# Strassen pairs of the FFNs: U2, U3 and P5 + P3 accumulate in PSUM, with ScalarE's copies in between, in place of VectorE's sums

## The reference, cut to what matters

```
def swiglu(x, w_gate, w_up, w_down):
    return (jax.nn.silu(x @ w_gate) * (x @ w_up)) @ w_down
x = x + FFN_RESIDUAL * swiglu(rms_norm(x, g[0]), ffn_w_gate[layer, 0], ffn_w_up[layer, 0], ffn_w_down[layer, 0])
```

## Time and profile before

| | |
|---|---|
| median of 3 runs | 1956.07 us |
| span of the profiled execution | 1954.0 us; the page gives no other time of it |
| TensorE busy | 1948.1 us (100%) |
| VectorE busy | 1397.9 us (72%) |
| ScalarE busy | 851.6 us (44%) |
| GpSimd busy | 527.3 us (27%) |
| DMA | 265.92 MB, mean 136 GB/s |

### The profile page before, as it was taken

One profiled execution on the slowest core, in us unless ns is written; L12 is line 12 of the kernel. 1 busy time (PEld: TensorE's weight loads), 2 busy tenths in 40 slices (PEclk: granted clock), 3 DMA queues, 4 the chain that ended last, 5 costly groups with the idle time before them and its releaser, 6 DMA issues.

```text
span 1954.0 us, 28996 instructions
## 1 busy us (share of the span) xinstructions
PE 1948.1 (100%) x11722; PEld 1707.3 (87%) x11722; DVE 1397.9 (72%) x1882; ACT 851.6 (44%) x1230; POOL 527.3 (27%) x394
## 2 busy tenths in 40 slices
PE   9999999999999999999999999999999999999999
PEld 7999998877789999988999998877777888999997
DVE  7877776554588877768877776773458657877773
ACT  6443333535554344345433444442546345333431
POOL 1322222142223322223322322200015413322221
PEclk9999999999999999999999999999999999999999
DMA  6556663351346666545666653232200235666653
GB/s 211 155 164 171 173 168 95 119 181 55 88 126 176 174 172 167 147 129 145 178 166 172 181 151 114 97 96 88 76 1 1 87 116 160 177 173 168 178 141 107
DMA packets 112469, 265.92 MB, mean 136 GB/s; under 512 B 10321, under 2 KB 22865, under 8 KB 112337
## 3 DMA queue, kind: packets, MB, share of 16 engines
q1 hardware_dynamic: 92336, 225.72, 35.3%
q0 software_dynamic: 19856, 38.28, 12.5%
q10 hardware_dynamic: 144, 0.09, 0.0%
HBM read 259.32 MB, written 4.72 MB: 135 GB/s over the span
## 4 chain that ended last, share of the span: by engine, by line
PE 98%; DVE 1%; DMA 0%; issue 0%; ACT 0%; SPq 0%; POOL 0%; DVEq 0%
PE BANKS L656 12%; PE BANKS L658 12%; PE BANKS L657 12%; PE BANKS L579 11%; PE BANKS L580 11%; PE BANKS L581 11%; PE BANKS L709 6%; PE BANKS L710 6%; PE BANKS L711 6%; PE BANKS L1022 2%; PE BANKS L850 1%; PE BANKS L852 1%; PE BANKS L851 1%; PE BANKS L999 1%; PE BANKS L1005 1%; PE BANKS L813 1%
## 5 line engine op out<-in xcount | busy, mean ns | idle before, releaser
L656 PE MATMUL BANKS<-BF,ASH 128*128 128x256 f32 x876 | 248.0, 283 | 0.0
L658 PE MATMUL BANKS<-BF,ASL 128*128 128x256 f32 x876 | 247.9, 283 | 0.0
L657 PE MATMUL BANKS<-BFL,ASH 128*128 128x256 f32 x876 | 247.9, 283 | 0.0
L579 PE MATMUL BANKS<-XH,HI 128*128 128x512 f32 x624 | 245.7, 394 | 0.7 <-DVE XL L1593 0.3
L1657 DVE TENSOR_TENSOR LO<-RING,HI 128x1024 fp32r<-128x1024 f32 (+2 forms) x204 | 216.3, 1060 | 41.2 <-ACT HI L1160 39.9
L580 PE MATMUL BANKS<-XL,HI 128*128 128x512 f32 x624 | 243.2, 390 | 0.0
L581 PE MATMUL BANKS<-XH,LO 128*128 128x512 f32 x624 | 243.0, 389 | 0.0
L1173 ACT ACTIVATE TMP<-TMP 128x512 f32<-128x512 f32 x88 | 55.7, 633 | 406.4 <-DVE TMP L1686 406.4
L2262 POOL TENSOR_TENSOR TMP<-TMP,RSTD 128x512 f32<-128x512 f32 x88 | 132.0, 1499 | 365.3 <-ACT TMP L1173 365.3
L2254 POOL DMA_DIRECT2D ASR<-gu_dram x73 | 88.1, 1219 | 387.5 <-DMA ASR<-gu_dram 381.5
L709 PE MATMUL BANKS<-HH,DHI 128*128 128x512 f32 x488 | 190.7, 391 | 0.0
(11 more groups left out here) (249 smaller groups left out, 4875.5 us busy)
## 6 DMA issues: line engine op xcount, KB each, us to landing
RING<-gu_dram SPq DMA_DIRECT2D x174, 512.0 KB, 3.9
ASR<-gu_dram SPq DMA_DIRECT2D x146, 256.0 KB, 2.9
ASR<-gu_dram POOLq DMA_DIRECT2D x73, 512.0 KB, 6.9
DRAW<-down_dram SPq DMA_DIRECT2D x40, 512.0 KB, 3.7
RING<-oin_dram SPq DMA_DIRECT2D x32, 512.0 KB, 3.5
RING<-down_dram SPq DMA_DIRECT2D x32, 384.0 KB, 3.2
DRAW<-down_dram SPq DMA_DIRECT2D x24, 384.0 KB, 3.7
RING<-ein_dram SPq DMA_DIRECT2D x16, 512.0 KB, 3.6
```

Source lines behind the costliest of these rows:

```text
L579: pe.matmul(PS[bank][:], HI[j][:, c], hi(k), start=(n == 0), stop=False)
L656: pe.matmul(out, w_hi[:, c], x_hi(k), start=(k == 0), stop=False)
L657: pe.matmul(out, w_hi[:, c], x_lo(k), start=False, stop=False)
L658: last = pe.matmul(out, w_lo[:, c], x_hi(k), start=False, stop=(k == 3))
```

## The change

What it does:

- TensorE's order becomes P1, P5, P6, P2, P7, P3, P4. P1, P6 and P7 accumulate in one half bank, bank 4 or 5 by turns with p (`chain`), so that it holds P1, then U2, then U3. P5 starts the up bank's high half, and P3 accumulates on it. P2 goes to the same bank's low half without a start flag. P4 goes as before to the gate bank's low half.
- ScalarE copies the half bank after each step: P1 to MID[0] (as before), U2 to MID[1] (`copy_six`), U3 to MID[2] (`copy_seven`); and P5 from the up bank's high half to the gate bank's high half (`copy_five`), from PSUM to PSUM.
- TensorE waits for P1's copy before P6 (as before, now one product behind P1 and not three), for P5's copy before P2, and for U2's copy before P7. It no longer waits for VectorE's `mid_five` before P4, nor for the last pair's `mid_three` before P1; instead P1 waits for U3's copy of two pairs ago (in an FFN's first pair, of the last one).
- VectorE's `mid_two`, `mid_five` and `mid_three` are gone. `whole_up` adds MID[0:2] = (P1, U2) to the up bank, `whole_gate` adds MID[2] = U3 to the gate bank.
- ScalarE's order for a middle pair becomes: copy of P1, split of up weights, copy of P5, split of gate weights, copy of U2, two splits of sums, copy of U3, early split, silu, copy of h. In an FFN's first pair the copy of P5 stands behind the copy of the previous pair's h, and early split and up weights' split stand ahead of the copy of U2. In a pair behind one without an early part, the copy of P5 comes ahead of the copy of h and the copy of U2 behind it and behind the up weights' split.
- SyncE's load of the pair sums' inputs two pairs ahead waits for P7 of the pair (`seven_done`) instead of P5, since P7 is now the later of the two that read the tiles it overwrites.
- XH and XL, BF and BFL, ASH and ASL are views of common tiles at the same addresses as before. MID has six half tiles instead of four, and the mixer region grows from 34 to 35 tiles.

```diff
@@ SyncE, block_ffn
-                        sp.wait_ge(five_done, block_count(f, n // 2 - 2) + 1)
+                        sp.wait_ge(seven_done, block_count(f, n // 2 - 2) + 1)
                         load_pair(f, n // 2)
@@ TensorE, block_ffn
                 def block(p):
...
+                    chain = PS[4 + p % 2][:, 0:TH_]
...
-                    if g:
-                        pe.wait_ge(mid_made, 5 * g - 2)
-                    product(PS[5][:, low], HI[up][:, left], LO[up][:, left], plain(0, 0)).then_inc(one_done, 1)
+                    if g >= 2:
+                        pe.wait_ge(seven_copied, g if p == PLAIN[f] else g - 1)
+                    product(chain, HI[up][:, left], LO[up][:, left], plain(0, 0), True, True).then_inc(one_done, 1)
                     pe.wait_ge(sum_lo, 2 * g + 1)
-                    product(PS[4][:, low], *summed(p, 0), form(1)).then_inc(seven_done, 1)
-                    product(gate_bank[:, high], *summed(p, 1), form(0)).then_inc(five_done, 1)
+                    product(up_bank[:, high], *summed(p, 1), form(0), True, True).then_inc(five_done, 1)
                     pe.wait_ge(one_copied, g + 1)
                     pe.wait_ge(sum_lo, 2 * g + 2)
-                    product(PS[5][:, low], *summed(p, 2), form(2)).then_inc(six_done, 1)
-                    product(up_bank[:, low], HI[up][:, right], LO[up][:, right], plain(4, 0)).then_inc(unit_done, 1)
-                    product(up_bank[:, high], *summed(p, 3), plain(4, 1)).then_inc(three_done, 1)
-                    pe.wait_ge(mid_made, 5 * g + 2)
+                    product(chain, *summed(p, 2), form(2), False, True).then_inc(six_done, 1)
+                    pe.wait_ge(five_copied, g + 1)
+                    product(up_bank[:, low], HI[up][:, right], LO[up][:, right], plain(4, 0),
+                            False, True).then_inc(unit_done, 1)
+                    pe.wait_ge(six_copied, g + 1)
+                    product(chain, *summed(p, 0), form(1), False, True).then_inc(seven_done, 1)
+                    product(up_bank[:, high], *summed(p, 3), plain(4, 1), False, True).then_inc(three_done, 1)
                     pe.wait_ge(lo_ready, n + 2)
                     product(gate_bank[:, low], HI[gate][:, right], LO[gate][:, right], form(3)).then_inc(unit_done, 1)
@@ ScalarE, block_ffn
                     act.wait_ge(one_done, g + 1)
                     if g:
-                        act.wait_ge(mid_made, 5 * g - 1)
-                    act.activation(MID[:, 0, :], PS[5][:, 0:TH_], ACT.Copy).then_inc(one_copied, 1)
+                        act.wait_ge(up_added, g)
+                    act.activation(MID[:, 0, :], PS[4 + p % 2][:, 0:TH_], ACT.Copy).then_inc(one_copied, 1)
+
+                def copy_five(p):
+                    up_bank, gate_bank = block_banks(p)
+                    act.wait_ge(five_done, block_count(f, p) + 1)
+                    act.activation(PS[gate_bank][:, TH_:T], PS[up_bank][:, TH_:T], ACT.Copy).then_inc(five_copied, 1)
+
+                def copy_six(p):
+                    act.wait_ge(six_done, block_count(f, p) + 1)
+                    act.activation(MID[:, 1, :], PS[4 + p % 2][:, 0:TH_], ACT.Copy).then_inc(six_copied, 1)
+
+                def copy_seven(p):
+                    g = block_count(f, p)
+                    act.wait_ge(seven_done, g + 1)
+                    if g:
+                        act.wait_ge(gate_added, g)
+                    act.activation(MID[:, 2, :], PS[4 + p % 2][:, 0:TH_], ACT.Copy).then_inc(seven_copied, 1)
...
                     copy_one(p)
                     if p == first:
                         h_high(p - 1)
+                        copy_five(p)
                         early_split(p)
                     elif not has_early(f, p - 1):
+                        copy_five(p)
                         h_high(p - 1)
                     if nxt:
                         split(2 * nxt, whole)
-                        split(2 * nxt + 1, right)
+                        if p > first and has_early(f, p - 1):
+                            copy_five(p)
+                            split(2 * nxt + 1, right)
+                            copy_six(p)
+                        else:
+                            copy_six(p)
+                            split(2 * nxt + 1, right)
                         sums_split(nxt, 0)
                         sums_split(nxt, 1)
                     else:
                         split(NU, late)
+                        if has_early(f, p - 1):
+                            copy_five(p)
+                        copy_six(p)
                         split(NU + 1, late)
+                    copy_seven(p)
                     if p == ALONE[f]:
                         early_split(p + 1)
@@ VectorE, block_ffn
-                def mid_two(p):
...
-                def mid_five(p):
...
-                def mid_three(p):
...
                 def whole_up(p):
...
-                    dve.wait_ge(mid_made, 5 * g + 2)
+                    dve.wait_ge(six_copied, g + 1)
                     dve.wait_ge(three_done, g + 1)
-                    dve.tensor_tensor(bank, bank, MID[:, 0:2, :], ALU.add).then_inc(mid_made, 1)
+                    dve.tensor_tensor(bank, bank, MID[:, 0:2, :], ALU.add).then_inc(up_added, 1)
...
                         if leads(f, p):
-                            if p > first:
-                                early_split(p)
-                            mid_two(p)
-                            mid_five(p)
-                            mid_three(p)
-                            if p == first:
-                                early_split(p)
+                            early_split(p)
                         sums_second(nxt)
                         sums_third(nxt)
                         dve.wait_ge(sum_made, 2 * block_count(f, nxt) + 2)
                         split(2 * nxt, whole)
-                        if not leads(f, p):
-                            mid_two(p)
-                            mid_five(p)
-                            mid_three(p)
                         if not leads(f, p):
                             early_split(p)
```

More of the change, by code:

```diff
@@ L189, in trunk @@
         hr0 = region("h_region", 16 * TB)
-        e0 = region("mixer_region", 34 * TB)
+        e0 = region("mixer_region", 35 * TB)
         tmp0 = region("tmp_region", 8 * TB)
@@ L201, in trunk @@
         TMP = at("TMP", [P, 8, T], tmp0, 0)
-        XH = at("XH", [P, KX, T], xr0, 0, F32R)
-        XL = at("XL", [P, KX, T], xr0, 8 * TB, F32R)
+        XHL = at("XHL", [P, 2, KX, T], xr0, 0, F32R)
+        XH, XL = XHL[:, 0], XHL[:, 1]
         HH = at("HH", [P, 8, T], hr0, 0, F32R)
@@ L247, in trunk @@
         WT = [TMP[:, 0, :], TMP[:, 1, 0:3 * P], WT2[:], TMP[:, 1, 3 * P:T]]
-        BF = at("BF", [P, 4, 4, TH_], e0, 0, F32R)
+        FORMS = at("FORMS", [P, 2, 2, 16 * TH_], e0, 0, F32R)
+        BFHL = FORMS[:, :, 0, :].rearrange("p m (k i t) -> p m k i t", k=4, i=4)
+        BF, BFL = BFHL[:, 0], BFHL[:, 1]
+        ASL, ASH = (FORMS[:, m, 1, :].rearrange("p (b i c) -> p b i c", b=2, i=4) for m in range(2))
         BFR = at("BFR", [P, 4, 4, TH_], e0, 16 * TB)
-        BFL = at("BFL", [P, 4, 4, TH_], e0, 16 * TB, F32R)
         ASR = at("ASR", [P, 2, 4, T], e0, 8 * TB)
-        ASL = at("ASL", [P, 2, 4, T], e0, 8 * TB, F32R)
-        ASH = at("ASH", [P, 2, 4, T], e0, 24 * TB, F32R)
-        MID = at("MID", [P, 4, TH_], e0, 32 * TB)
+        MID = at("MID", [P, 6, TH_], e0, 32 * TB)
         DRAW = at("DRAW", [P, KMAX * P], tmp0, 4 * TB)
@@ L317, in trunk @@
             sem(n) for n in ("one_done", "five_done", "six_done", "seven_done"))
-        one_copied, mid_made, three_done = (sem(n) for n in ("one_copied", "mid_made", "three_done"))
+        one_copied, five_copied, six_copied, seven_copied, three_done = (
+            sem(n) for n in ("one_copied", "five_copied", "six_copied", "seven_copied", "three_done"))
+        up_added, gate_added = sem("up_added"), sem("gate_added")
         form_in, form_step, form_made, form_hi, form_lo = (
@@ L650, in block_ffn, with product @@
                 base = 4 * q0
-                def product(out, w_hi, w_lo, tokens):
-                    x_hi, x_lo = tokens
+                def product(out, w_hi, w_lo, tokens, fresh=True, shares=False):
                     for k in range(4):
                         c = slice(k * P, k * P + P)
-                        pe.matmul(out, w_hi[:, c], x_hi(k), start=(k == 0), stop=False)
-                        pe.matmul(out, w_hi[:, c], x_lo(k), start=False, stop=False)
-                        last = pe.matmul(out, w_lo[:, c], x_hi(k), start=False, stop=(k == 3))
+                        both = tokens(k)
+                        pe.matmul(out, w_hi[:, c], both[:, 0, :], start=(fresh and k == 0), stop=False,
+                                  skip_group_check=shares)
+                        pe.matmul(out, w_hi[:, c], both[:, 1, :], start=False, stop=False, skip_group_check=shares)
```

(4 more changed lines are left out.)

33 lines of the change are left out of this document (6 added, 27 removed).

## The result

The changed kernel takes 1972.12 us (median of 4 runs, 1969.86 to 1972.36) against 1955.62 (4 runs, 1954.97 to 1956.20). The ratio is 1.0083, 95% interval 1.0069 to 1.0097: slower, 0.9 us under the prediction. The profiled execution of the changed kernel has a span of 1970.2 us in a time of 1971.9, against 1954.0 before: 16.2 us more, where the sum said 16.8. The granted clock is 1.0 in both.

The account below looks back on a forecast made before the run. TensorE was taken as the bound, busy 1948.1 of 1954.0 us. Terms -0.35 + 3.2 + 8.0 + 5.0 + 1 = 16.8 us made the span 1970.8 and, with 2.1 around it, the time 1973; range 1964 to 1986.

Parts of the forecast that it names:

- the one stall: TensorE's only wait over 0.3 us in the old pairs, for VectorE's sum of P5: removing it gives back 0.35 us.
- The middle pairs: Down split behind U3's copy makes the first down weight load 0.065 us late in 49 pairs: 3.2 us.
- The first pairs: First pair of each FFN: P1's, P5's and U2's copies late on ScalarE; 2.7, 3.2, 2.0 and 0.1, sum 8.0 us.
- Pairs 16 and 21: Five pairs behind one without a down part: P1's and U2's copies late, 2 x 1.07 + 3 x 0.94 = 5.0 us.
- The late load: SyncE's pair load goes out at 7.4 instead of 4.51 us into the pair; cost 1 us, ends 0 and 4.
- the rival of late pairs: Pair-load landings 3.1 us later than the median in most pairs cost 0.5 us in each of 62: 2004 us; chance 0.08.
- The copy into PSUM: ScalarE's copy of P5, not shown in the old trace: taken as 0.38 us, bounded by 0.28 and 0.70.
- The down split: Rival: VectorE's down split costs 0.27 us in each of 49 pairs, +10 on the sum: 1983 us; chance 0.10.
- the faster case: Rival: 219 fewer VectorE PSUM reads take 3 ns off each of 6132 matmuls, -18 us; chance 0.02.
- the rule against the row: TensorE pulling weight loads past waiting matmuls would shorten each stall by 0.12 us: sum about 12, time 1968; row opposes it.

Follow-up runs that it names:

- the adds alone: Changed kernel plus three unused 128x256 adds on VectorE ahead of its early down split, with no extra wait before that split: 1971.77 us.
- the wait-alone kernel: Changed kernel plus one always-met wait on VectorE between its weight split and early down split, no adds: 1974.59 us.
- the late load alone: Kernel before the change, with only SyncE's pair load waiting for the pair's fifth product instead of the third: 1957.35 us.
- three moves in one engine's order: Changed kernel, ScalarE reordered: down split before U3's copy (middle pairs), P5's and U2's copies before h (first pairs), U2's before h (pairs 16, 21): 1959.51 us.
- the first version of mine: Changed kernel plus three unused 128x256 adds on VectorE ahead of its early down split, each followed by a wait on VectorE's own semaphore: 1977.50 us.

## Why the prediction was right

**Nothing to win.** The removed sums gave back the one stall, 0.3 us by the pitch, and no more. That VectorE's freed time has no other worth in the 58 pairs that got the adds is shown by the adds alone, 1971.77 against 1972.12: with three adds back, the time is the same within its spread.

**The middle pairs** came as worked out: the split at t = 7.67 (151.18 - 143.51), the low part at 8.75, the load at 153.54 for 153.46. It rested on a 0.04 step between engines, and the wait-alone kernel shows how thin such a term is: 0.07 more in that step made it 0.16.

**The first pairs** were 6.5 instead of 8.0, and this is the mis-sized term. 0.9 of the 1.5 is FFN 1's P1 copy, 0.39 late, not 1.33: by t it started at 2.73 (584.47 - 581.74) and in the earlier trace rows at 3.67. The two steps behind were 1.31 and 0.54, for 1.33 and 0.52. FFN 2 had 0, 1.16 and 0.54 for 0.13, 1.33 and 0.54. I had taken one execution's state for a constant. What sets it is VectorE's second low part of the weight sums, through the gate product and the silu: it ended 2.51 us into FFN 1's first pair before the change and 1.56 after. In the seven other kernels whose P1 copy stands in that place behind the silu (all but the one that moves it and the late load alone), it ended 1.70 to 3.31 us into the pair, and the waits of the second and third product together were 0.5 to 2.1 us, in each case within 0.02 of that end less 1.17. Why VectorE comes earlier or later against TensorE I did not settle.

**Pairs 16 and 21** came out at 1.03 and 0.92 for 1.07 and 0.94.

**The late load** was 1.6 in the profiled execution and 2.2 in the median when made alone, for 1 with ends 0 and 4. Its landing rose only to 7.6, so the rival of late pairs was out. The term was mis-sized by treating the five late landings as the whole distribution.

**The rivals.** The copy into PSUM took 0.37, as the nearest row had it. The down split did not take more than counted (1.23 at most). TensorE's pitch stayed at 0.12 with 219 reads of PSUM fewer on VectorE, so the faster case had no ground; it had also left out that ScalarE's three copies in each pair are 219 reads more. As to the rule against the row: the three stalled loads shown above sat idle until their copy's end and came 0.04 to 0.06 behind it, and the sum counted from the loads (16.8) is nearer to the measured 16.2 than the 12 of the rule. Counting from the loads is right to 0.02 us a stall: in FFN 1's first pair they are 0.39, 1.31 and 0.54 late, and the pair is 2.22 longer.

The closeness is in part luck, since the errors cancel: the first pairs were 1.5 too high, the loads and middle pairs 0.9 too low. The difference between time and span is 1.7, not 2.1.

## What to carry to other kernels

Work moved to an engine with 44% load is not free if a third engine waits for each piece: ask what stands ahead of it in that engine's program, at the stage's starts and wherever the rhythm changes, and place it by the time when it is needed. Here 8 pairs of 73 carried 11.4 of the 16.2 us, and three moves in one engine's order gave back 12.6 us of the median. An engine at 72% is not worth relieving where nobody waits for it. Where TensorE did wait for VectorE, in FFN 1's first pair, it was for low parts that stand ahead of the removed sums. Of two waits, write the one that decides first. And an experiment that adds work must not add a wait with it: the first version of mine measured the wait.

## What the hardware showed that I had not expected

- A wait that was met long ago costs 0.07 us if it stands in the code ahead of the wait that decides: VectorE then starts 0.10 us after ScalarE's end instead of 0.03 (57 of 62 against 53 of 53). Behind the deciding wait it costs nothing (ScalarE's copy of P1, 52 of 52). In a chain that the bounding engine waits for, 0.07 us a pair came to 0.09 in the pitch. That the order of the waits is what decides is read from these rows; no run swapped two waits.
- ScalarE's copy from PSUM to PSUM takes 0.368 us and from PSUM to SBUF 0.384 (medians of 73). The Trainium skill (ScalarE: Activation LUTs, "Step-by-step: what each stage is for") calls PSUM the lower-latency port; the trace agrees, by 0.016 us.
- A stall costs what its weight load is late, not what its first matmul is late. A late first matmul starts with its load and not 0.12 us behind it, but the matmul behind it comes 0.22 and not 0.12 later. So by the matmul starts a stall of 0.5 to 1.3 us is followed by 0.09 or 0.10 more in the next product.
- GpSimd's accumulating DMA lands in 7.6 us at the median instead of 6.9 when the pair load goes out 2.9 us later in the pair (7.4 with the later load alone). SyncE's 512 KB weight loads land later too, 4.5 instead of 3.9 us, also with the later load alone. This fits transfers that overlap; I did not separate them.
